# Fourier stage with folded channels and twice-folded time, and differential scores in three blocks of 384 keys

## The reference

```
gate, (na_q, na_k, na_v, na_z, f_u, f_z, d_q, d_k, d_v, d_z, g) = mixer_input(xs, c, norm_g[l], w_mod[l], b_mod[l], w_in[l])
o_na = from_heads(neighbourhood_attention(qa, ka, va, cache_na_k[:, l], cache_na_v[:, l], na_rpb[l]))
o_f  = fourier_mix(f_u, fnet_w[l])
o_d  = from_heads(diff_attention(qd, kd, vd, lam, diff_subln_g[l], lam_init))
y    = merge_branches(g, (o_na, o_f, o_d), (na_z, f_z, d_z), w_branch[l], w_out[l])
xs   = xs + gate * y
```

## Time and profile before

| | |
|---|---|
| median of 3 runs | 2941.22 us (2939.51 to 2941.58) |
| span of the profiled execution | 2938.6 us, 44082 instructions |
| PE busy | 2877.4 us, 98% of the span |
| DVE, ACT, POOL busy | 1330.6, 1076.5, 614.0 us |
| PE's share of the chain that ended last | 89% |
| Fourier stage of layer 0, u0 to w3 | 527 to 699 us |
| differential stage of layer 0, all units and steps | 699 to 1230 us |

### The profile page before, as it was taken

The page is one execution under the profiler, slowest core; times in us unless marked ns, Lnnn a source line. Parts: engine busy times, 40 slices in busy tenths (PEclk is TensorE's granted clock), DMA queues, the critical chain, the costliest instruction groups (busy, mean ns, idle before and its releaser), DMA issues.

```text
span 2938.6 us, 44082 instructions
## 1 busy us (share of the span) xinstructions
PE 2877.4 (98%) x18396; PEld 2756.4 (94%) x18396; DVE 1330.6 (45%) x2291; ACT 1076.5 (37%) x1947; POOL 614.0 (21%) x312
## 2 busy tenths in 40 slices
PE   6999999999999999999999999999999999999998
PEld 5999999999999999999999999999999989899997
DVE  4343443123557575446344434421146567554543
ACT  4333333221444544422343333323133444443231
POOL 0221221122221212122431221211221121211242
PEclk9999999999999999999999999999999999999999
DMA  5332224102111102254421121220211111215532
GB/s 224 102 110 82 102 90 137 67 15 78 42 47 47 48 32 94 80 203 141 133 79 65 66 82 39 94 83 22 70 41 45 44 48 47 78 51 183 165 110 94
DMA packets 84278, 248.55 MB, mean 85 GB/s; under 512 B 9201, under 2 KB 30193, under 8 KB 83057
## 3 DMA queue, kind: packets, MB, share of 16 engines
q1 hardware_dynamic: 84080, 245.74, 24.5%
HBM read 191.71 MB, written 54.00 MB: 84 GB/s over the span
## 4 chain that ended last, share of the span: by engine, by line
PE 89%; DVE 5%; ACT 2%; DMA 2%; issue 1%; SPq 1%; DVEq 0%; POOL 0%; POOLq 0%; ACTq 0%
PE ps L730 44%; PE ps L713 18%; PE ps L823 6%; PE ps L769 6%; PE ps L900 3%; PE ps L1041 3%; PE ps L1032 2%; PE ps L961 2%; PE ps L888 2%; PE ps L943 1%; DVE e L1839 1%; DVE stat L1822 1%; ACT e L1435 1%; DMA wmod<-w_mod 1%; DVE aTl L1846 1%
## 5 line engine op out<-in xcount | busy, mean ns | idle before, releaser
L730 PE MATMUL ps<-hhi,whi 128*128 128x384 f32 x2640 | 916.3, 347 | 5.7 <-DVE obuf L1854 3.3
L730 PE MATMUL ps<-hhi,wlo 128*128 128x384 f32 x2640 | 886.3, 336 | 0.0
L730 PE MATMUL ps<-hlo,whi 128*128 128x384 f32 x2640 | 884.1, 335 | 0.0
L1956 POOL TENSOR_TENSOR wlo<-wraw,whi 128x1024 fp32r<-128x1024 f32 (+1 forms) x188 | 415.8, 2212 | 2063.6 <-ACT whi L1127 2063.5
L730 PEld LDWEIGHTS ps<-hhi,whi 128*128 128x128 f32 x2640 | 500.0, 189 | 24.1 <-issue 7.3
L730 PEld LDWEIGHTS ps<-hlo,whi 128*128 128x128 f32 x2640 | 497.1, 188 | 0.9
L730 PEld LDWEIGHTS ps<-hhi,wlo 128*128 128x128 f32 x2640 | 495.9, 188 | 0.0
L1127 ACT ACTIVATE whi<-wraw 128x1024 fp32r<-128x1024 f32 (+1 forms) x188 | 174.5, 928 | 229.9 <-PE ps L713 209.3
L1444 ACT ACTIVATE aTh<-ps 128x512 fp32r<-128x512 f32 (+1 forms) x200 | 96.5, 482 | 278.4 <-PE ps L1032 278.4
L1691 DVE TENSOR_TENSOR ptl<-ps,pth 128x512 fp32r<-128x512 f32 (+1 forms) x144 | 82.1, 611 | 246.8 <-ACT pth L1301 246.6
L1822 DVE TENSOR_REDUCE stat<-ps 128x1 f32<-128x1152 f32 x144 | 176.5, 1231 | 16.9 <-PE ps L769 16.0
(11 more groups left out here) (199 smaller groups left out, 4835.8 us busy)
## 6 DMA issues: line engine op xcount, KB each, us to landing
wraw<-w_in SPq DMA_DIRECT2D x128, 512.0 KB, 4.2
gates_dram<-gst SPq DMA_DIRECT2D x48, 576.0 KB, 3.0
gth<-gates_dram SPq DMA_DIRECT2D x48, 576.0 KB, 4.9
mraw<-w_mod SPq DMA_DIRECT2D x32, 512.0 KB, 3.8
wraw<-w_branch SPq DMA_DIRECT2D x48, 256.0 KB, 2.8
bias<-rpb SPq DMA_DIRECT2D x8, 1280.0 KB, 6.0
outs_dram<-obuf SPq DMA_DIRECT2D x16, 576.0 KB, 3.9
oraw<-outs_dram SPq DMA_DIRECT2D x16, 576.0 KB, 3.8
```

Source lines behind the costliest of these rows:

```text
L730: x = mm(ps[:, bank, 0:CH], a[:, s % 2, k, :], b[:, k, n * CH:(n + 1) * CH], start=(k == 0 and a is whi and b is hhi), stop=(k == KT - 1 a ...
L1956: g_.tensor_tensor(lo[:, 0:kt, :], wraw[:, n % 2, 0:kt, :], hi[:, 0:kt, :].bitcast(F32), ALU.subtract).then_inc(S.w_lo, 1)
```

## The change

**Channels.** `tab_c` has 128 columns instead of 256: cosines of 65 frequencies and sines of 63, which is all that differs, since the transform of real data mirrors. **Time.** ACT now writes group g to `uT` in two halves of 513 tokens, the second one running backwards, so that a token t and its mirror have known places; `pair(g, 0)` and `pair(g, 1)` each multiply four token tiles with 128 columns, and `pair(g, 2)` holds the context tile and a matmul of 2 columns for tokens 0 and 512. DVE folds twice: sum and difference (`xpm`), and from these the stacked operand `xst`, in which cosine and sine channels share the 128 rows. `over_tokens` then needs 2 outputs of 4 matmuls. The missing mirrored half of the channels is restored in the map that follows: `fnet_w` arrives as two row orders, 8 blocks instead of 4 for each chunk (512 KB instead of 256), and DVE joins them in `wraw` (`joined`) ahead of ACT's split. The first-token term is added as a bias by ACT and DVE when they write `ft`, where ACT now writes half of `ft` itself. There are two tables `tab_t` instead of four, and a small table `fsigns` is loaded at the start.

**Scores.** The differential scores of a tile are three blocks of 384 keys; the context tile's scores (128 keys) are computed right behind those of t = 7, in columns 384 to 511 of the first bank of each map, in both attention stages; the step t = 7 no longer has scores in it. Maxima and exponentials read the 3 by 384 blocks.

The diff, cut to its core:

```diff
-                    sp.dma_start(wraw[:, n % 2, 0:chunk_k(c), :], weight(*c)).then_inc(w_load[n % 2], 16)
+                    kt = KT if c[0] == "w" else chunk_k(c)
+                    sp.dma_start(wraw[:, n % 2, 0:kt, :], weight(*c)).then_inc(w_load[n % 2], 16)
...
-                        if t == LT:
-                            x = score([(e, ps[:, e, 0:P]) for e in range(2)], t, TL + PAST, TK)
-                        elif t == LT - 1:
-                            x = score([(e, ps[:, e, 0:3 * P]) for e in range(2)], t, TL - 2 * P, TL + PAST)
+                        if t == LT - 1:
+                            score([(e, ps[:, e, 0:3 * P]) for e in range(2)], t, TL - 2 * P, TL + PAST)
+                            x = score([(e, ps[:, e, 3 * P:4 * P]) for e in range(2)], LT, TL + PAST, TK)
...
-                        pe.wait_ge(S.tab_load, 96 * (l + 1))
+                        pe.wait_ge(S.tab_load, 64 * (l + 1))
                         pe.wait_ge(*evacuated("u", l, "fn", g))
-                    if j < 2 and g:
-                        pe.wait_ge(*((S.q_done, 2 * n), (S.f_ctx, n))[j])
-                    if j >= 2:
-                        pe.wait_ge(S.folded, n * 5 + j - 1)
-                    for i, t in enumerate((j, j + 4) if j < 4 else (8,)):
-                        x = mm(ps[:, 6 + j % 2, 256 * i:256 * i + 256], uT[:, g % 2, t * P:(t + 1) * P],
-                               tab_c[:].rearrange("p a b -> p (a b)"), start=True, stop=True)
+                    if j == 1 and g:
+                        pe.wait_ge(S.f_ctx, n)
+                    if j == 2:
+                        pe.wait_ge(S.folded, n * 3 + 1)
+                        mm(ps[:, 6, 0:P], uT[:, g % 2, 2 * UH:], tab_c[:], start=True, stop=True)
+                        mm(ps[:, 6, P:P + 2], tab_c[:], uT[:, g % 2, 0:2 * UH:UH], start=True, stop=True
+                           ).then_inc(S.u_pair, 1)
+                        return
+                    up, down = 1 + P * j, TL // 4 + 1 + P * j
+                    for i, at in enumerate((up, down, UH + up, UH + down)):
+                        x = mm(ps[:, 6 + j, i * P:(i + 1) * P], uT[:, g % 2, at:at + P], tab_c[:], start=True, stop=True)
                     x.then_inc(S.u_pair, 1)
...
+                def tokens_free(g):
+                    pe.wait_ge(S.q_done, 2 * (l * HEADS + g))
+                    pe.wait_ge(S.f_ctx, l * HEADS + g)
...
-                    pe.wait_ge(S.folded, n * 5 + 4)
-                    for i, bank in enumerate((3, 4, 5, 6)):
-                        if bank == 6:
-                            pe.wait_ge(S.folded, n * 5 + 5)
-                        x_in, part = ((xsum, 0), (xsum, 1), (xdif, 0), (xdif, 1))[i]
-                        width = (HK + 1) if i < 2 else HK
-                        for j in range(4):
-                            x = mm(ps[:, bank, 0:width], x_in[:, j, part, :], tab_t[j][:, i, 0:width],
-                                   start=(j == 0), stop=(j == 3))
+                    pe.wait_ge(S.folded, n * 3 + 3)
+                    for odd in range(2):
+                        width = HK if odd else HK + 1
+                        for j in range(2):
+                            for part in range(2):
+                                x = mm(ps[:, 3 + odd, 0:width], xst[:, j, odd, part, :], tab_t[j][:, 2 * odd + part, 0:width],
+                                       start=(j == 0 and part == 0), stop=(j == 1 and part == 1))
                         x.then_inc(S.x_done, 1)
...
-                            for b, (k0, k1) in enumerate(((0, 512), (512, 1024), (1024, 1152))):
-                                x = score([(m, ps[:, 3 * m + b, 0:k1 - k0]) for m in range(2)], t, k0, k1)
+                        for b in range(NC):
+                            x = score([(m, ps[:, 3 * m + b, 0:CH]) for m in range(2)], t, b * CH, (b + 1) * CH)
+                        if t == LT - 1:
+                            x = score([(m, ps[:, 3 * m, CH:CH + P]) for m in range(2)], LT, TL + PAST, TK)
                         x.then_inc(S.df_s, 2)
...
-                        if t < LT:
+                        if t < LT - 1:
...
+                    if SPLIT[s][0] == "w":
+                        act.wait_ge(S.w_joined, SPLIT[s][1] * HEADS + SPLIT[s][3] + 1)
...
-                    grid = uT[:, g % 2, 0:TL].rearrange("p (r c) -> p c r", c=GW)
+                    both = uT[:, g % 2, 0:2 * UH].rearrange("p (h t) -> p h t", t=UH)
+                    up = both[:, :, 0:TL // 4].rearrange("p h (r c) -> p c h r", c=GW)
+                    down = both[:, :, TL // 2:TL // 4:-1].rearrange("p h (r c) -> p c h r", c=GW)
                     for i, (a, b) in enumerate(((0, 24), (24, 48), (48, GW))):
-                        fn(grid[:, a:b], u_in[:, i, 0:(b - a) * GH].rearrange("p (c r) -> p c r", r=GH), ACT.Copy)
-                    fn(uT[:, g % 2, TL:], u_in[:, 2, TL - 2 * CH:], ACT.Copy).then_inc(S.act_evac, 1)
+                        src = u_in[:, i, 0:(b - a) * GH].rearrange("p (c h s r) -> p c h s r", h=2, s=2, r=4)
+                        fn(up[:, a:b], src[:, :, :, 0], ACT.Copy)
+                        fn(down[:, a:b], src[:, :, :, 1], ACT.Copy)
+                    fn(both[:, :, TL // 4], u_in[:, 0, 4:GH:8], ACT.Copy)
+                    fn(uT[:, g % 2, 2 * UH:], u_in[:, 2, TL - 2 * CH:], ACT.Copy).then_inc(S.act_evac, 1)
...
+                    for j in range(2):
+                        act.wait_ge(S.u_pair, 3 * (l * HEADS + g) + j + 1)
+                        fn(xab[j][:], ps[:, 6 + j, 0:2 * P], ACT.Copy).then_inc(S.pair_copied, 1)
...
+                    act.wait_ge(S.x_done, 3 * n + 1)
+                    fn(ft[:, 0:TL // 2 + 1:2], ps[:, 3, 0:HK + 1], ACT.Identity, bias=first_t[:, 2:3]).then_inc(S.q_even, 1)
+                    act.wait_ge(S.q_done, 2 * n + 1)
+                    fn(ft[:, 1:TL // 2:2], ps[:, 4, 0:HK], ACT.Identity, bias=first_t[:, 3:4])
...
+                        dve.wait_ge(S.pair_copied, 2 * n + j + 1)
+                        if g == 0 and j == 0:
+                            v.memset(xst[:, :, :, 0, COS:], 0.0)
+                            v.memset(xst[:, :, :, 1, 0:COS], 0.0)
+                            v.memset(xctx[:, 0, COS:], 0.0)
+                            v.memset(xctx[:, 1, 0:COS], 0.0)
+                        if g and j == 0:
+                            dve.wait_ge(S.x_done, 3 * n)
+                        v.tensor_tensor(xpm[:, j, 0], xab[j][:], ps[:, 6 + j, 2 * P:], ALU.add)
+                        v.tensor_tensor(xpm[:, j, 1], xab[j][:], ps[:, 6 + j, 2 * P:], ALU.subtract)
+                        dve.drain()
+                        for odd in range(2):
+                            x, y = xpm[:, j, odd, 0:P], xpm[:, j, odd, P:]
+                            v.tensor_tensor(xst[:, j, odd, 0, 0:COS], x[:, 0:COS], y[:, 0:COS], ALU.subtract if odd else ALU.add)
+                            z = v.tensor_tensor(xst[:, j, odd, 1, COS:], x[:, COS:], y[:, COS:], ALU.add if odd else ALU.subtract)
+                        z.then_inc(S.folded, 1)
+                    dve.wait_ge(S.u_pair, 3 * n + 3)
+                    if g:
+                        dve.wait_ge(S.f_ctx, n)
+                    v.tensor_copy(xctx[:, 0, 0:COS], ps[:, 6, 0:COS])
+                    v.tensor_copy(xctx[:, 1, COS:], ps[:, 6, COS:P])
+                    v.tensor_scalar(first_t[:, 0:2], ps[:, 6, P:P + 2], signs[:, 2:3], None, ALU.mult)
+                    dve.drain()
+                    v.tensor_tensor(first_t[:, 2:3], first_t[:, 0:1], first_t[:, 1:2], ALU.add)
+                    v.tensor_tensor(first_t[:, 3:4], first_t[:, 0:1], first_t[:, 1:2], ALU.subtract).then_inc(S.folded, 1)
...
+                def joined(m):
+                    n = CHUNK["w", l, "fn", m]
+                    dve.wait_ge(*loaded_no(n))
+                    v.scalar_tensor_tensor(out=wraw[:, n % 2, 0:BK, :], in0=wraw[:, n % 2, BK:, :], scalar=signs[:, 0:1],
+                                           in1=wraw[:, n % 2, 0:BK, :], op0=ALU.mult, op1=ALU.add).then_inc(S.w_joined, 1)
...
+                joined(0)
                 fn_gate(2)
+                joined(1)
                 fn_gate(3)
                 for m in range(HEADS):
+                    if m < 2:
+                        joined(2 + m)
```

134 lines of the change are left out of this document (63 added, 71 removed).

## The result

The changed kernel takes **2910.07 us** (median of 4 runs, 2909.03 to 2910.77). The kernel before, run beside it, takes 2940.63 (4 runs, 2939.51 to 2941.58). The ratio is 0.9896, 95% interval 0.9884 to 0.9908: 30.6 us less, where 44.05 were forecast.

What follows compares the result with a forecast made beforehand. PE, busy for 98% of the span, was taken to bound the kernel. Terms -41.2 + 2.8 + 0.45 - 1.5 - 4.6 = -44.05 us took 2941.2 to 2897.2 us, range 2888 to 2910.

Steps and rivals of the forecast that it cites:

- PE's work in the Fourier stage: Fourier groups: pairs and context 1.69 us less, token matmuls 3.46 less, over 8 groups 41.2 us less.
- Neither waits: Fourier groups after the first: fold needs 2.0 of 4.0 us, `forward` 2.0 to 2.5 of 3.9; no PE wait.
- The first group: First Fourier group of each layer: PE's wait grows from 1.1 to about 2.5 us, 2.8 us more in all.
- What makes the first group late: First Fourier group: weight load, ACT's split and copy, DVE's fold, in unchanged order; `uT` writing and DVE's additions delay release.
- The fetch of `fnet_w` and the join: Weight chunks in the Fourier stage: 4.2 us load and 0.7 us join fit into 19 us of lead; charged nothing.
- Scores: Both attention stages: 1.5 us less in the neighbourhood stage, 4.6 us less in the differential stage.
- The start: Setup loads: one small table more ahead of the loads on the chain, 0.45 us more.
- Rival (a): Shorter Fourier cycle exposes ACT and DVE, PE waits 1 to 2 us in each of 8 groups; 2905 to 2913, chance 0.14.

Runs made afterwards that it cites:

- e6: Changed kernel with ACT copying the first group's pairs before the weight split, and POOL's `flo` held until DVE's next second folds; 2895.28 us, ratio 0.9848.
- e10: e6 with `mul_a` of the next layer computed behind the first `xT`, as in e9; 2889.84 us, ratio 0.9832.
- e2: Kernel before with only the Fourier part of the change and its loads, without the scores' edits; 2912.17 us, ratio 0.9906.
- e4: Changed kernel, in group 0 ACT copies the pairs before it rounds the next weight chunk; 2896.78 us, ratio 0.9854.
- e5: Changed kernel with the small table `fsigns` fetched just ahead of layer 0's Fourier tables, not at the start; 2908.17 us, ratio 0.9895.
- e9: Changed kernel with the next layer's small products `mul_a` computed behind the first `xT`, not ahead of it; 2903.87 us, ratio 0.988.
- e3: Changed kernel, POOL makes a group's low output half only when DVE has folded the next group's second pair; 2903.4 us, ratio 0.9871.
- e8: e6 with DVE zeroing a quarter of `xst` 13 times instead of once in group 0, as a delay; 2906.31 us, ratio 0.9885.
- e1: Kernel before with only the edits to the scores; 2932.88 us, ratio 0.9978.

## Why the prediction was off

The direction and most of the size were right (30.6 of 44.05 us), but the time came out 12.9 us above the forecast, and 0.07 above the upper end of its range, 2910. Two steps failed: that no group but the first waits, and that the first group's waits were priced as if the clock stayed at 1.00. Step by step:

- **PE's work in the Fourier stage (-41.2): right.** In e6 and e10, where nothing waits, the stages take 43.4 us less. That is 41.2 and the 2.2 of the first groups' old waits. A float32 matmul of 128 columns paces at half of one with 256, as I had read from the earlier trace rows: eight L951 instructions take 0.90 us.
- **"Neither waits", in the other groups: the step that failed.** I gave the fold chain 2.0 us against 4.0 of cover, with DVE's small operations 0.13 us apart. They are 0.13 apart when POOL is idle. With both inputs in SBUF, one of them is held through POOL's `flo`, 2.92 us; PE then waits in the six other groups, 3.9 us in all, and some 1.6 us more is lost with these waits: the kernels that have them (changed, e2, e4, e5, e9) are longer by 1.5 to 1.9 us in these stages than e6 with its waits and clock added, those without (e3, e8) by 0.3 at most. That makes 5.5 us where the prediction had nothing. The added operations are the first of this chain that take both inputs from SBUF, which was to be seen in the diff. Removing the hold gave 7.0 us of stage (e3 against the changed kernel), 1.6 of it by the clock.
- **The first group (+2.8): the wait well sized, its price too low.** 3.04 and 2.79 us for a forecast 2.5. But I priced all at a clock of 1.00. The clock costs 3.0 us more in layer 0 and 1.7 in layer 1. With 5.8 of waits that makes 10.5 us for both layers against 5.0.
- **What makes the first group late: right, but for one step.** The order load, split, copy, fold is that of the prediction, the four MEMSETs take 0.71 us for a forecast 0.5; the step that was not in it is 0.4 us of hold on L1763. Taking the split out from ahead of the copies removes the whole wait (e4).
- **The fetch of `fnet_w` and the join: right.** No wait of PE for a w chunk.
- **Scores (-6.1): right in sum,** 7.3 by the median of e1 and 5.3 in the stages of its profiled execution, with the stages' shares off by 1 to 2 us. In the changed kernel the stretch with the differential stage shows only 1.4 us. One cause is the same hold: in layer 1 `e` (L1880), an operation on two SBUF tiles, starts 0.12 us after a split of POOL's, takes 3.49 us, and PE waits 1.71 for it.
- **The start (+0.45): too low for this execution,** 3.6, and it goes with the clock, which rose 5.0 us later than in before. I can't assign it to the change.
- **Left out altogether: places that the change doesn't touch.** At the layers' boundary 2.3 us of wait and about 1.5 of clock came in because the second `mul_a` lost to POOL's split (e6, e9, e10).

Rival (a) gives the right time, 2905 to 2913, and a wait in every group, but that is luck, since its reason is not the one found: DVE and ACT have time enough, and DVE is kept from using it. The Fourier stages' shortfall of 10.9 us (38.4 forecast, 27.5 found) is accounted for, 5.5 by each failed step. What remains unexplained is 2.1 to 2.9 us less from layer 1's branch projection to the end in every kernel with the Fourier edits.

## What to carry to other kernels

When a change puts an operation with two SBUF inputs on DVE's path to PE, don't price it by its length: look at what POOL runs in the same microseconds, and add POOL's longest instruction, or order POOL behind it. The trace of before shows how that went for the operations of this kind that are already there. An operation whose result isn't needed yet belongs behind the urgent ones for the same reason. A wait of PE of 3 us cost 3 us here and up to 3 more by the clock, so it pays to remove the last one in a stretch; and after an edit, compare also the stages that it doesn't touch, since a gain can be lost there by phase alone.
